# Neighbourhood-attention bias tables in an encoder block: key rows turned round, slots loaded in 13 transfers, tables built in the first stage

## The chip, the cores and the metric

One core of a Trainium2 chip runs the whole program in one launch. The metric is the device time in microseconds (us) of one execution; several executions are timed and their median is taken. A change of less than about 0.2% can't be told from none.

## What is computed

One layer of a bidirectional encoder on a prompt (1024 tokens) and a sample (512 tokens), each with 16 learned meta tokens before it. What matters here is the first attention group: 8 heads, tokens on a grid 64 wide, each query sees a window of 8 grid rows by 16 columns, with a learned bias by row and column offset, and the meta tokens.

```python
def _neighbourhood_attention(q, k, v, rpb, meta_bias):
    rows = n_real // GRID_W
    kh = min(NA_MAX_KH, rows)
    row_start = jnp.clip(r_idx - kh // 2, 0, rows - kh)
    col_idx = jnp.clip(c_idx - NA_KW // 2, 0, GRID_W - NA_KW)[:, None] + jnp.arange(NA_KW)
    col_off = col_idx - c_idx[:, None] + NA_KW - 1
    ...
    def row_fn(args):
        qr, r, rs = args
        ...
        row_off = rs + jnp.arange(kh) - r + NA_MAX_KH - 1
        bias = rpb[:, row_off[:, None, None], col_off[None]]
        ...
        s_loc = s_loc.astype(jnp.float32) * scale + bias[None]
        p = jax.nn.softmax(jnp.concatenate([s_loc, s_met], axis=-1), axis=-1)

def _layer(...):
    h = _rmsnorm(x, norm_mix)
    proj = h @ w_in
    ...    # neighbourhood heads | differential heads, output projection, residual
    x = x + _expert_choice_ffn(_rmsnorm(x, norm_ffn), ...)    # 16 experts, top-k tokens each
```

## The kernel before

Every engine has its instruction stream written out by hand, with semaphores between them; SyncE (SP) issues all transfers of the attention stages, in program order, and each of them is at least one instruction of its stream.

**Stage A (0 to 75 us).** The tokens come in 12 tiles of 128 rows (and one of 32), in pairs, in a loop: SP waits on `xn_ready` until both tiles of the pair before are normed, then loads `xt`; ScalarE squares, GpSimd makes the root, VectorE scales, TensorE turns the tiles round, ScalarE and VectorE split them into the parts `hT_hi` and `hT_lo`.

**Projections.** A unit is a pair of heads; units 0 to 3 are neighbourhood heads, 4 to 7 differential ones. `project` (L1427) makes V, Q and K of a unit in 12 chunks of 24 matmuls, in two PSUM banks by turns; `evac` (a helper at L650) copies each chunk out on ScalarE. Its weights come by `load_w` (L446), in three parts j = 0, 1, 2, and each part is split by `split_wq` on ScalarE (`wq_hi`) and then on VectorE (`wq_lo`, L980). Unit 0 is projected alone; each later unit during the attention of the unit before. On ScalarE `split_wq(1, 0)` stands between chunks 7 and 8 of unit 0; on ScalarE and VectorE `split_wq(1, 1)` stands ahead of the first attention step.

**Neighbourhood steps.** A unit has 13 steps (`NA`): three column groups `ct` (steps 0 to 2, 3 to 8, 9 to 11), each block of 16 query columns with three kinds of 8 grid rows, and a step for the meta tokens. In step s TensorE makes scores (L1471), half a chunk of the next unit's projection, turns the step before round (L1494, L1495), the other half chunk, and weights the values (L1508, L1515). VectorE adds the bias and finds the minimum of the negated sum (L1091, `nmax`), which waits for the bias slot; ScalarE takes the exponential (L751). In unit 3 VectorE also rotates the columns of unit 4 (L1036), from copies `swp` that SP issues (`swap_halves`, L524).

**Bias.** A slot (`bias[:, i % 2]`) holds, for one unit and column group, the bias of 128 queries against 384, 384 and 256 keys and 16 meta tokens. It is loaded from a DRAM table `window_bias` (8 heads x 3 groups x 16 columns x 32 rows x 32), by 31 transfers (L492) and three of `meta_bias` (L511, 128 partitions x 2 x 16 floats each). The table is filled with the mask value (L463, three transfers) and then written by 78 transfers of pieces of 16 floats from `rpb` (L481), after the last tile of stage A. Queries of 8 rows need 8 shifted row ranges; with key rows rising each shift is a transfer of its own.

Of the kernel before, what the change touches and what calls it, by code (L numbers as in the profile page):

```python
# [73 lines left out]
TROWS = 32  # L74
VCH = 24
SLOT_DMAS = 31 + 3
# [50 lines left out]
def build(nc, x_all, w_in, w_out, w_router, w_gate, w_up, w_down, rpb, meta_bias, lambdas, vecs,  # L127
# [7 lines left out]
    bias_h = nc.dram_tensor("window_bias", (NA_HEADS, 3, QW, TROWS * WIN), f32, kind="Internal")  # L135
    bias_d = bias_h.ap()

    ctx = ExitStack()
    with ctx:
# [165 lines left out]
        fill_ready, fill_in, diag_in = sem("fill_ready"), sem("fill_in"), sem("diag_in")  # L305
        mask_ready, bias_in = sem("mask_ready"), [sem(f"bias_in{b}") for b in range(2)]
# [76 lines left out]
        def window(tile, f, kind, block):  # L383

            base = (0, 4 * GRID_W, N_PROMPT)[kind]
            rows = tile[f, base:base + KROWS[kind] * GRID_W].rearrange("p (r k) -> p r k", k=GRID_W)
            return rows[:, :, WSTART[block]:WSTART[block] + WIN]
# [20 lines left out]
        def key_chunks(kind, block):  # L408

            first = (0, 1, 4)[kind]  # L410
            return [4 * (first + j) + block for j in range(KCOLS[kind] // P)]
# [17 lines left out]
        def _(sp):  # L429
# [6 lines left out]
            sp.dma_start(cos[:, :], rope[0]).then_inc(const_in, 16)  # L436
            sp.dma_start(sin[:, :], rope[1]).then_inc(const_in, 16)
            sp.dma_start(pmask[:, :], pair_mask).then_inc(const_in, 16)
# [12 lines left out]
            with sp.Fori(0, PAIRS) as i:  # L451
                for b in range(2):
                    sp.wait_ge(xn_ready, 2 * i + CREDIT)
                    sp.dma_start(xt[:, b, :], x_all[bass.ds((2 * i + b) * P, P), :]).then_inc(x_in[b], 16)
            sp.wait_ge(xn_ready, 2 * PAIRS + CREDIT)
            sp.dma_start(xt[0:TAIL, 0, :], x_all[N_REAL:NTOK, :]).then_inc(x_in[0], 16)


            flat = NA_HEADS * 3 * QW * TROWS * WIN
            sp.wait_ge(fill_ready, 1)  # L460
            for n in range(flat // (P * 1024)):
                dst = bass.AP(tensor=bias_h, offset=n * P * 1024, ap=[[1024, P], [1, 1024]])
                sp.dma_start(dst, mask_fill[:, :]).then_inc(fill_in, 16)  # L463
            sp.wait_ge(fill_in, 16 * (flat // (P * 1024)))
            CS = TROWS * WIN
            HS_ = 3 * QW * CS
            half = KW // 2
            runs = [(0, c, 1, 0, KW - 1 - c) for c in range(half)] + [(0, half, QW - half, 0, half - 1)]
            runs += [(1, 0, QW, 0, half - 1)]
            runs += [(2, 0, half + 1, half, half - 1)] + [(2, c, 1, KW, KW - 1 - c) for c in range(half + 1, QW)]  # L470
            for ct, c, n, k0, off in runs:
                for row0, nrow, roff in ((0, ROFF, 0), (ROFF + 1 + 3, KH, 3)):
                    dst0 = (ct * QW + c) * CS + row0 * WIN + k0
                    for h in range(NA_HEADS) if n > 1 else (None,):
                        if h is None:
                            src = bass.AP(tensor=rpb.tensor, offset=roff * COFF + off, ap=[[ROFF * COFF, NA_HEADS], [COFF, nrow], [1, KW]])
                            dst = bass.AP(tensor=bias_h, offset=dst0, ap=[[HS_, NA_HEADS], [WIN, nrow], [1, KW]])
                        else:
                            src = bass.AP(tensor=rpb.tensor, offset=(h * ROFF + roff) * COFF + off, ap=[[0, n], [COFF, nrow], [1, KW]])
                            dst = bass.AP(tensor=bias_h, offset=h * HS_ + dst0, ap=[[CS + 1, n], [WIN, nrow], [1, KW]])  # L480
# [58 lines left out]
            for i in range(2):  # L539
                load_bias(i)  # L540
# [1348 lines left out]
```

## Time and profile before

| | us |
|---|---|
| median of three runs | 3352.49 (3350.26 to 3354.61) |
| the profiled execution | 3356.26 |
| its span, first to last instruction | 3354.4 |

| engine | busy, us | share of the span |
|---|---|---|
| TensorE, matmuls | 3008.0 | 90% |
| VectorE | 1898.2 | 57% |
| ScalarE | 1475.6 | 44% |
| GpSimd | 171.3 | 5% |

The experts take the span from about 1200 us on, with TensorE busy 9 tenths or more in nearly every slice. The stages named above lie in the first 600 us. The table of 40 slices shows TensorE there at 3, 6 and 8 tenths in its first three slices of 84 us, then at 9; the granted clock of TensorE is below full in some of them. Read the waits for who waits for whom, then the timeline of each engine (start, duration, line, operation, and in brackets the idle time ahead with what ended it).

### The profile page before, as it was taken

To read this page: it belongs to the slowest core of one execution; us is meant where nothing else is said; L and a number is where in the kernel's file an instruction comes from. 1 tells how busy PE (TensorE), PEld (TensorE's weight loads), DVE (VectorE), ACT (ScalarE), POOL (GpSimd) and SP (SyncE) were. 2 spreads that over 40 slices of the span, in tenths; PEclk is the share of its full clock that TensorE was granted. 3 is DMA by queue.
4 is the path that set the end of the run, shared out by engine and by line. 5 is a ranking of instruction groups with operands and counts; after the bars stand their busy time and mean duration, and the time that the engine had idled before them with its cause. 6 is when DMAs were issued, how large, how long until landed. Compare 5 with 4: busy or idle time off the path is not lost.

```text
span 3354.4 us, 50481 instructions
## 1 busy us (share of the span) xinstructions
PE 3008.0 (90%) x19541; PEld 2809.8 (84%) x19541; DVE 1898.2 (57%) x2984; ACT 1475.6 (44%) x2422; POOL 171.3 (5%) x177
## 2 busy tenths in 40 slices
PE   3689998989898799179999999999999999999993
PEld 3678887768675577079999999999999999999993
DVE  5023223647567322856766676667667666766672
ACT  3023232323335222055655565556556555655562
POOL 1000000000000100000001000100100100000001
PEclk7889998989898789589999999999999999999996
DMA  4323332101001232077777787777777777877774
GB/s 131 56 57 73 73 73 55 30 27 34 21 23 59 85 125 97 3 233 234 236 228 237 224 249 222 237 233 232 234 232 239 224 237 228 248 220 234 237 218 171
DMA packets 649094, 529.21 MB, mean 158 GB/s; under 512 B 39792, under 2 KB 629904, under 8 KB 648880
## 3 DMA queue, kind: packets, MB, share of 16 engines
q1 hardware_dynamic: 640688, 500.53, 48.4%
q0 software_dynamic: 8192, 25.70, 3.9%
q8 instruction: 150, 2.46, 0.3%
q14 instruction: 64, 0.52, 0.0%
HBM read 473.45 MB, written 40.54 MB: 153 GB/s over the span
## 4 chain that ended last, share of the span: by engine, by line
PE 60%; issue 32%; DVE 3%; DMA 2%; POOL 1%; ACT 1%; SPq 0%; ACTq 0%; POOLq 0%; DVEq 0%
PE ps L1717 37%; PE ps L1718 17%; PE ps L1644 5%; DMA xt<-x_all_dram 1%; PE ps L1762 1%; DVE top_i L1285 1%; DVE top_v L1283 1%; DVE aff L1286 1%; PE ps L1711 1%; DMA raw<-w_up_dram 0%; PE ps L1662 0%; POOL rstd L1775 0%; DMA y_dram<-yo 0%; POOL rstd_d L1775 0%; DVE x L1225 0%
## 5 line engine op out<-in xcount | busy, mean ns | idle before, releaser
L1717 PE MATMUL ps<-xe,w_hi 128*128 128x392 f32 x4096 | 1195.3, 364 | 8.2 <-DVE xe L1328 8.2
L1718 PE MATMUL ps<-xe,w_lo 128*128 128x196 f32 x4096 | 1034.1, 252 | 0.0
L1315 DVE TENSOR_TENSOR w_lo<-raw,w_hi 128x2048 fp32r<-128x2048 f32 x384 | 875.8, 2284 | 11.3 <-ACT w_hi L650 11.3
L1718 PEld LDWEIGHTS ps<-xe,w_lo 128*128 128x128 f32 x4096 | 784.1, 191 | 0.0
L1717 PEld LDWEIGHTS ps<-xe,w_hi 128*128 128x128 f32 x4096 | 770.0, 188 | 8.5 <-DVE xe L1328 8.5
L650 ACT ACTIVATE w_hi<-raw 128x2048 fp32r<-128x2048 f32 x384 | 732.1, 1911 | 91.8 <-DMA raw<-w_gate_dram 75.1
L1717 PE MATMUL ps<-hid,w_hi 128*128 128x392 f32 x2048 | 609.4, 366 | 0.0
L1718 PE MATMUL ps<-hid,w_lo 128*128 128x196 f32 x2048 | 516.8, 252 | 0.0
L1718 PEld LDWEIGHTS ps<-hid,w_lo 128*128 128x128 f32 x2048 | 391.5, 191 | 0.0
L1717 PEld LDWEIGHTS ps<-hid,w_hi 128*128 128x128 f32 x2048 | 384.5, 188 | 0.0
L1348 DVE TENSOR_TENSOR gusum<-ps,part 128x392 f32<-128x392 f32 x256 | 145.0, 566 | 395.1 <-ACT part L650 395.1
L650 ACT ACTIVATE part<-ps 128x392 f32<-128x392 f32 x256 | 127.4, 498 | 511.3 <-PE ps L1718 511.3
L1427 PE MATMUL ps<-hT_hi,wq_hi 128*128 128x384 f32 (+1 forms) x768 | 287.1, 374 | 14.9 <-ACT kT L650 8.8
L1427 PE MATMUL ps<-hT_lo,wq_hi 128*128 128x384 f32 (+1 forms) x768 | 268.7, 350 | 0.0
L1427 PE MATMUL ps<-hT_hi,wq_lo 128*128 128x384 f32 (+1 forms) x768 | 268.2, 349 | 0.0
L779 ACT ACTIVATE e_df<-e_df,nmax 128x1040 f32<-128x1040 f32 (+3 forms) x112 | 112.3, 1004 | 214.7 <-DVE e_df L1164 214.7
L1427 PEld LDWEIGHTS ps<-hT_hi,wq_hi 128*128 128x128 f32 x768 | 149.9, 195 | 46.8 <-issue 28.6
L1369 DVE TENSOR_TENSOR yT<-ps,y_part 128x196 f32<-128x196 f32 x128 | 46.3, 361 | 198.1 <-ACT y_part L650 196.4
L650 ACT ACTIVATE y_part<-ps 128x196 f32<-128x196 f32 x128 | 42.3, 331 | 249.1 <-PE ps L1718 249.1
L1427 PEld LDWEIGHTS ps<-hT_lo,wq_hi 128*128 128x128 f32 x768 | 150.7, 196 | 0.3
L1427 PEld LDWEIGHTS ps<-hT_hi,wq_lo 128*128 128x128 f32 x768 | 149.9, 195 | 0.5
L1164 DVE TENSOR_SCALAR_CACHE_REDUCE e_df<-ps,nmm 128x1024 f32<-128x1024 f32 (+3 forms) x112 | 117.8, 1088 | 45.5 <-PE ps L1552 45.5
(166 smaller groups left out, 3212.2 us busy)
## 6 DMA issues: line engine op xcount, KB each, us to landing
raw<-w_gate_dram SPq DMA_DIRECT2D x128, 1024.0 KB, 5.3
raw<-w_up_dram SPq DMA_DIRECT2D x128, 1024.0 KB, 5.3
raw<-w_down_dram SPq DMA_DIRECT2D x128, 1024.0 KB, 5.5
wqkv<-w_in_dram SPq DMA_DIRECT2D x24, 512.0 KB, 4.0
xt<-x_all_dram SPq DMA_DIRECT2D x12, 512.0 KB, 4.2
v_na<-v SPq DMA_DIRECT2D x64, 96.0 KB, 2.3
mixed_heads<-mix SPq DMA_DIRECT2D x96, 64.0 KB
mixs<-mixed_heads SPq DMA_DIRECT2D x12, 512.0 KB, 4.8
```

The source lines that it names most:

```text
L650: return act.activation(out, in_, ACT.Copy, scale=scale)
L779: act.activation(e_df[0:rows, s % 2, c, 0:w], e_df[0:rows, s % 2, c, 0:w], ACT.Exp, bias=nmax[0:rows, s % 2, c:c + 1], scale=-1.0, accum_o ...
L1164: dve.tensor_scalar(e_df[0:rows, s % 2, c, 0:kt * P], ps[0:rows, 2 * c * BANK:2 * c * BANK + kt * P], -1.0, nmm[0:rows, c, t:t + 1], ALU.m ...
L1283: own.mark(dve.max(top, aff[:, :]))
L1285: own.mark(dve.max_index(top_i[:, 8 * r:8 * r + 8], top, aff[:, :]))
L1315: dve.tensor_tensor(w_lo[:, n % NW, :], raw[:, n % NRAW, :], w_hi[:, n % NW, :].bitcast(f32), ALU.subtract).then_inc(lo_done, 1)
L1348: dve.tensor_tensor(gusum[:, m % 2, :, :], src[:, :, 0:SLOTS], part[:, m % 2, :, :], ALU.add).then_inc(sum_done, 1)
L1369: dve.tensor_tensor(yT[:, d, :], ps[:, off:off + SLOTS], y_part[:, d % 2, :], ALU.add).then_inc(yT_done, 1)
L1427: ins = pe.matmul(ps[:, off:off + c1 - c0], wt[:, p, k, :], x[:, k, c0:c1], start=(k == 0 and j == 0), stop=(k == KD - 1 and j == 2))
L1644: ins = pe.matmul(ps[0:rows, off:off + 512], x[:, b, k, 0:rows], w[:, k, n * 512:(n + 1) * 512], start=(k == 0 and j == 0), stop=(k == KD ...
L1717: pe.matmul(out, w_hi[:, slot, cols], x.rearrange("p h n -> p (h n)"), start=first, stop=False)
L1718: return pe.matmul(out[:, 0:SLOTS], w_lo[:, slot, cols], x[:, 0, :], start=False, stop=last)
```

## The change

- K of the neighbourhood units is kept with its grid rows falling (`turned`): ScalarE copies a K chunk row by row, 6 copies of 64 columns in place of one of 384, with one more of 32 in the last chunk. Windows, value rows and `key_chunks` follow. The host turns `rpb`'s rows round and pads them.
- The shifts of 8 query rows are then a constant step in one table, so that a slot takes 5 pieces x 2 heads = 10 transfers and the 3 of `meta_bias`: 13 in place of 34.
- Two DRAM tables, `bias_full` and `bias_band`, take the place of `window_bias`. They are filled by 4 transfers ahead of the second pair of tiles, written by 5 transfers of 16-float pieces (3 after the third pair's loads, 2 after the fourth's) and one copy from table to table (after the last pair's).
- The masked part of a slot that no transfer writes is set once by a VectorE `memset` of both slots (128 x 4288) at the end of stage A.
- SP's order: the first pair's tiles ahead of `cos`, `sin`, `pmask` and the first weights; the loop of pairs is written out; both bias slots ahead of `load_w(1, 0)` and `load_windows(0, ...)` instead of behind them. VectorE and TensorE wait for 3 constants, VectorE for the other three later.

```diff
-SLOT_DMAS = 31 + 3
+SLOT_DMAS = 2 * 5 + 3
...
+            x_pair(0)
+            sp.dma_start(cos[:, :], rope[0]).then_inc(tables_in, 16)
+            sp.dma_start(sin[:, :], rope[1]).then_inc(tables_in, 16)
+            sp.dma_start(pmask[:, :], pair_mask).then_inc(tables_in, 16)
...
+            sp.wait_ge(fill_ready, 1)
+            for h, n, rows in FILLS:
+                dst = bass.AP(tensor=h, offset=n * 1024, ap=[[1024, rows], [1, 1024]])
+                sp.dma_start(dst, mask_fill[0:rows, :]).then_inc(fill_in, 16)
+            def diagonal(ct, c, n, k0, off):
+                src = bass.AP(tensor=rpb.tensor, offset=PADR * COFF + off, ap=[[0, n], [COFF, NA_HEADS * ROFF], [1, KW]])
...
+            half = KW // 2
+            for i in range(1, PAIRS):
+                x_pair(i)
+                if i == 2:
+                    sp.wait_ge(fill_in, 16 * len(FILLS))
+                    edge(0, 0, half, 0)
+                    diagonal(0, half, QW - half, 0, half - 1)
+                    diagonal(1, 0, QW, 0, half - 1)
+                if i == 3:
+                    diagonal(2, 0, half + 1, half, half - 1)
+                    edge(2, half + 1, QW - half - 1, KW)
+                if i == 5:
+                    sp.wait_ge(diag_in, 16 * DIAGS)
...
+                    sp.dma_start(dst, src).then_inc(band_in, 16)
...
+                def piece(table, rows, at_col, r0, nr, row0, nrow):
+                    for a in range(2):
...
+                        src = bass.AP(tensor=table, offset=(ct * QW * rows + first + row0) * WIN,
+                                      ap=[[WIN, nr], [rows * WIN, QW], [1, nrow * WIN]])
+                        dst = bass.AP(tensor=bias, offset=(QW * r0 * 2 + b) * 2 * SLOT + a * (SLOT + N_META) + at_col,
+                                      ap=[[4 * SLOT, nr * QW], [1, nrow * WIN]])
+                        sp.dma_start(dst, src).then_inc(bias_in[b], 16)
...
+                full(BOFF[0] + 4 * WIN, 0, 4, 0, KH)
+                band(BOFF[0], 4, 4, 0, 12)
+                band(BOFF[1], 0, 5, 0, 12)
+                full(BOFF[1], 5, 3, 5, KH)
+                full(BOFF[2], 0, QR, 0, KH)
...
+            sp.wait_ge(band_in, 16)
+            sp.wait_ge(bias_clear, 1)
+            for i in range(2):
+                load_bias(i)
             load_w(1, 0)
             for block in range(4):
                 load_windows(0, block)
-            for i in range(2):
-                load_bias(i)
             for j in range(1, 3):
                 load_w(1, j)
...
+                elif which == 1 and uu < UNITS:
+                    for r in range(6 * c, 6 * c + 6):
+                        at_k = turned(r) * GRID_W
+                        ins = copy(kTs[uu % 2][:, at_k:at_k + GRID_W],
+                                   ps[:, off + (r - 6 * c) * GRID_W:off + (r - 6 * c + 1) * GRID_W])
...
+            dve.memset(bias[:, :, :], MASKED).then_inc(bias_clear, 1)
+            dve.wait_ge(tables_in, 16 * 3)
```

How the change moves the instructions, in three places. SP at the start of the program, before (`mask_fill` and `rpb` pieces stand behind all tiles):

```order
L435 DMA lam_51<-lambdas_dram 128x256
L436 DMA cos<-rope_dram 128x1040
L437 DMA sin<-rope_dram 128x1040
L438 DMA pmask<-pair_mask_dram 32x128
L446 DMA wqkv<-w_in_dram 128x8x128 x3
...
L454 DMA xt<-x_all_dram 128x1024
...
L456 DMA xt<-x_all_dram 32x1024
L463 DMA window_bias<-mask_fill 128x1024 x3
L481 DMA window_bias<-rpb_dram 8x15x16
L481 DMA window_bias<-rpb_dram 8x8x16
```

The same place now:

```order
L452 DMA xt<-x_all_dram 128x1024 x2
...
L465 DMA wqkv<-w_in_dram 128x8x128 x3
...
L452 DMA xt<-x_all_dram 128x1024 x4
L489 DMA bias_full<-rpb_dram 8x127x16
L480 DMA bias_full<-rpb_dram 8x120x16
L480 DMA bias_full<-rpb_dram 16x120x16
L452 DMA xt<-x_all_dram 128x1024 x2
L480 DMA bias_full<-rpb_dram 9x120x16
L489 DMA bias_full<-rpb_dram 7x126x16
L452 DMA xt<-x_all_dram 128x1024 x4
L508 DMA bias_band<-bias_full 384x1x256
```

78 small transfers behind the tiles have become 5 larger ones and a copy between them. SP between stage A and the first attention step, before (31 rows of L492 in each slot; `v_87` is the value tile):

```order
L446 DMA wqkv<-w_in_dram 128x8x128
L533 DMA v_na<-v_87 32x6x128 x16
L492 DMA bias<-window_bias 16x2x256
L492 DMA bias<-window_bias 16x2x128
L492 DMA bias<-window_bias 16x2x384
...
L511 DMA bias<-meta_bias_dram 128x2x16 x3
...
L511 DMA bias<-meta_bias_dram 128x2x16 x3
L446 DMA wqkv<-w_in_dram 128x8x128 x2
L567 DMA mixed_heads<-mix 8x16x128
```

The same place now:

```order
L524 DMA bias<-bias_full 64x1x256 x2
L524 DMA bias<-bias_band 64x1x384 x2
L524 DMA bias<-bias_band 80x1x384 x2
L524 DMA bias<-bias_full 48x1x256 x2
L524 DMA bias<-bias_full 128x1x256 x2
L541 DMA bias<-meta_bias_dram 128x2x16 x3
...
L541 DMA bias<-meta_bias_dram 128x2x16 x3
L465 DMA wqkv<-w_in_dram 128x8x128
L564 DMA v_na<-v_87 32x6x128 x16
L465 DMA wqkv<-w_in_dram 128x8x128 x2
L600 DMA mixed_heads<-mix 8x16x128
```

The last two parts of unit 1's weights stood behind 68 bias transfers and now stand behind the value windows alone. ScalarE at the end of unit 0's projection, before:

```order
L650 ACTIVATE qT_78<-ps 128x32
L650 ACTIVATE wq_hi<-wqkv 128x512 x2
L650 ACTIVATE kT_80<-ps 128x384 x3
L650 ACTIVATE kT_80<-ps 128x416
L650 ACTIVATE wq_hi<-wqkv 128x512 x2
L751 ACTIVATE e_na,ssum<-e_na,nmax 128x400 x2
```

The same place now:

```order
L683 ACTIVATE qT_78<-ps 128x32
L683 ACTIVATE wq_hi<-wqkv 128x512 x2
L683 ACTIVATE kT_80<-ps 128x64 x24
L683 ACTIVATE kT_80<-ps 128x32
L683 ACTIVATE wq_hi<-wqkv 128x512 x2
L792 ACTIVATE e_na,ssum<-e_na,nmax 128x400 x2
```

Nothing changes its place there; four copies have become 25.

## Rows read from the trace of the kernel before

**Rows 1.** Waits, 70 to 200 us: engine, line, releaser; total us, times, longest us.

```profile
DVE wq_lo L980 <- ACT wq_hi L650: 77.9, 2, 49.4
ACT wq_hi L650 <- DMA wqkv<-w_in_dram: 52.8, 2, 37.8
PE ps L1471 <- DVE nmax L1091: 35.5, 1, 35.5
```

**Rows 2.** Timeline of SP, 0 to 200 us: start, us, line, transfer, count.

```profile
68.27 54.75 SPq L481 DMA_DIRECT2D window_bias<-rpb_dram  x78
124.44 0.41 SPq L446 DMA_DIRECT2D wqkv<-w_in_dram  x1
124.89 10.54 SPq L533 DMA_DIRECT2D v_na<-v  x16
135.48 15.86 SPq L492 DMA_DIRECT2D bias<-window_bias  x31
151.37 1.45 SPq L511 DMA_DIRECT2D bias<-meta_bias_dram  x3
152.87 14.46 SPq L492 DMA_DIRECT2D bias<-window_bias  x31
...
168.86 1.09 SPq L446 DMA_DIRECT2D wqkv<-w_in_dram  x2
```

**Rows 3.** Timeline of ScalarE: chunk copies of unit 0's projection.

```profile
108.55 0.55 ACT L650 ACTIVATE qT<-ps 128x256 f32<-128x256 f32 x2 [3.66 <-PE ps L1427]
113.10 0.58 ACT L650 ACTIVATE qT<-ps 128x384 f32<-128x384 f32 x2 [4.00 <-PE ps L1427]
...
141.11 0.52 ACT L650 ACTIVATE kT<-ps 128x416 f32<-128x416 f32 x1 [4.06 <-PE ps L1427]
```

**Rows 4.** Timeline of TensorE: projection's start and restart, scores of steps 0 to 3.

```profile
74.88 0.69 PE L1427 MATMUL ps<-hT_hi,wq_hi 128*128 128x384 f32 x1 [6.06 <-DVE hT_lo L973]
...
130.34 0.66 PE L1427 MATMUL ps<-hT_hi,wq_hi 128*128 128x384 f32 x1 [8.85 <-ACT kT L650]
...
141.68 0.92 PE L1471 MATMUL ps<-kT,qT 64*128 64x384 f32 x4 [0.61 <-ACT kT L650]
...
182.59 1.65 PE L1471 MATMUL ps<-kT,qT 64*128 64x384 f32 x4 [35.46 <-DVE nmax L1091]
...
193.79 0.70 PE L1471 MATMUL ps<-kT,qT 64*128 64x256 f32 x4
...
201.94 0.92 PE L1471 MATMUL ps<-kT,qT 64*128 64x384 f32 x4
```

**Rows 5.** Packets moved in 160:165, 533:538, 90:100 and 62.8:68.3 us, in that order.

```profile
DMA packets 917, 0.66 MB, mean 132 GB/s; under 512 B 320, under 2 KB 917, under 8 KB 917
...
DMA packets 540, 0.03 MB, mean 7 GB/s; under 512 B 540, under 2 KB 540, under 8 KB 540
...
DMA packets 2913, 0.18 MB, mean 18 GB/s; under 512 B 2912, under 2 KB 2912, under 8 KB 2912
...
DMA packets 480, 1.70 MB, mean 310 GB/s; under 512 B 64, under 2 KB 64, under 8 KB 480
```

**Rows 6.** Group of ScalarE, 70 to 600 us, by shape: busy us, mean ns.

```profile
L650 ACT ACTIVATE qT<-ps 128x128 f32<-128x128 f32 x8 | 2.1, 262 | 4.2 <-PE ps L1427 4.2
```

**Rows 7.** Timelines of SP and TensorE around unit 3: bias slots 10 and 11, a wait.

```profile
480.97 16.46 SPq L492 DMA_DIRECT2D bias<-window_bias  x31
...
516.88 14.58 SPq L492 DMA_DIRECT2D bias<-window_bias  x31
...
545.50 0.76 PE L1508 MATMUL ps<-v_meta,et_meta 32*128 32x128 f32 x2 [12.04 <-DVE et_meta L1079]
```

**Rows 8.** Timelines of VectorE and ScalarE in stage A: the mask, two pairs' squares.

```profile
2.07 0.91 DVE L941 MEMSET mask_fill<- 128x1024 f32 x1 [0.18 <-issue]
...
15.56 1.06 ACT L660 ACTIVATE junk<-xt 128x1024 f32<-128x1024 f32 x1 [5.38 <-DMA xt<-x_all_dram]
...
23.97 1.06 ACT L660 ACTIVATE junk<-xt 128x1024 f32<-128x1024 f32 x1 [6.02 <-DMA xt<-x_all_dram]
```

More of the change, by code:

```diff
@@ L408, in key_chunks, with turned @@
         def key_chunks(kind, block):
-            first = (0, 1, 4)[kind]
-            return [4 * (first + j) + block for j in range(KCOLS[kind] // P)]
+            groups = ((2, 1, 0), (3, 2, 1), (5, 4))[kind]
+            return [4 * g + block for g in groups]
+        def turned(row):
+            return PT * 2 - 1 - row if row < PT * 2 else PT * 2 + FULL * 2 - 1 - row
+        FILLS = [(h, n, min(P, np_ - n)) for h, np_ in ((full_h, 3 * QW * FROWS * WIN // 1024),
+                                                        (band_h, 3 * QW * NA_HEADS * BROWS * WIN // 1024))
+                 for n in range(0, np_, P)]
+        DIAGS = 5
         first_of = [min(s for s, x in enumerate(NA) if x[0] == ct) for ct in range(3)] + [NS]
@@ L465, in _ @@
[L465 to L480, printed above, removed]
-                        sp.dma_start(dst, src).then_inc(diag_in, 16)
@@ L482, in _ @@
[L482 removed]
             def load_bias(i):
                 u, ct, b = i // 3, i % 3, i % 2
[L488 to L506 removed]
+                def piece(table, rows, at_col, r0, nr, row0, nrow):
+                    for a in range(2):
+                        h = 2 * u + a
+                        first = PADR + h * ROFF if table is full_h else h * BROWS
+                        src = bass.AP(tensor=table, offset=(ct * QW * rows + first + row0) * WIN,
[3 more added lines that the diff above has]
+                        sp.dma_start(dst, src).then_inc(bias_in[b], 16)
@@ L507, in load_bias, with full, band @@
+                def full(*args):
+                    piece(full_h, FROWS, *args)
+                def band(*args):
+                    piece(band_h, NA_HEADS * BROWS, *args)
+                full(BOFF[0] + 4 * WIN, 0, 4, 0, KH)
[3 more added lines that the diff above has]
+                full(BOFF[2], 0, QR, 0, KH)
                 for kind in range(3):
@@ L699, in evac @@
                     copy(vT[:, 0:c1 - c0], ps[:, off:off + c1 - c0]).then_inc(pj_evac, 1)
+                elif which == 1 and uu < UNITS:
[3 more added lines that the diff above has]
+                                   ps[:, off + (r - 6 * c) * GRID_W:off + (r - 6 * c + 1) * GRID_W])
+                    if c == 3:
+                        ins = copy(kTs[uu % 2][:, N_REAL:NTOK], ps[:, off + N_REAL - c0:off + NTOK - c0])
+                    ins.then_inc(pj_evac, 1)
                 elif which == 1:
@@ L1871 @@
         "w_down": a["w_down"][0],
-        "rpb": a["na_rpb"][0],
+        "rpb": np.concatenate([np.zeros((PADR, 31), np.float32), a["na_rpb"][0][:, ::-1].reshape(-1, 31),
+                               np.zeros((PADR, 31), np.float32)]),
         "meta_bias": a["na_meta_bias"][0],
```

72 lines of the change are left out of this document (31 added, 41 removed).

## The prediction

> **What bounds the kernel now.** Most of the span is the experts' part with TensorE busy, which the change doesn't touch. So I read only the first 600 us, from the waits to the timelines. The waits between 70 and 200 us show one long hole on TensorE: 35.5 us in one piece, before the scores of step 1, released by VectorE's `nmax`. VectorE itself waited 49.4 us in `wq_lo` for ScalarE, and ScalarE 37.8 us for `wqkv` [rows 1]. The bias is not what they wait for: it is a weight transfer. SP's timeline tells why it is late: 78 table pieces take SP 54.8 us, then come one weight part, 16 window loads (10.5 us), 68 bias transfers (two slots of 31 at about 15 us and 3 at 1.45), and only at 168.9 the last two weight parts [rows 2]. SP's issuing is the bound from 68 to 170 us. Unit 0's projection, which stopped for the first weight part, shows the same queue: 8.85 us idle ahead of chunk 10, since ScalarE could copy no chunk while it waited for the part issued at 124.4 [rows 3, 4].
>
> **The first stall, step by step.** Now both slots are issued before the weights. They can start when VectorE's memset is done. The projection started at 74.9 [rows 4]; the memset follows at about that time on VectorE. An own figure for its length comes from the mask's 1024 columns below: 4288/1024 x 0.91 = 3.8 us, so SP goes on at about 78.7. Nothing waits for VectorE there until the first V chunk is turned. Each slot is then 10 transfers at 15.86/31 = 0.51 us and 3 in 1.45, 6.6 us of SP [rows 2]. Data: a slot is 2 x (64x256 + 64x384 + 80x384 + 48x256 + 128x256) floats = 0.93 MB; with a backlog, slot data moved at 132 GB/s, that is 7.1 us; the 768 pieces of `meta_bias` go at 540 in 5 us, another 7.1 us [rows 5]. Two slots: 78.7 + 1.9 + 28.4 = 109 us. `load_w(1, 0)` is behind them and lands at about 112, before ScalarE has copied chunk 7 (113.1 + 0.6) [rows 3]. Its wait disappears. `load_w(1, 1)` waits for chunk 7 (113.1) and is behind the windows (from 100.7 when V is done, 10.5 us), so it lands at about 117, needed at 132. `load_w(1, 2)` goes out at 130, needed at step 2.
>
> TensorE then runs on from 121.5. A chunk of 416 columns takes 113.10 - 108.55 = 4.55 us at full clock [rows 3], one of 384 then 4.2, and chunks 10 and 11 end at 130.3 in place of 141.07: **10.8 us**, of which 8.85 is the idle time and 2 the half clock after it. Step 0's scores wait for the last K copy: six copies of 64 columns and one of 32. A copy of 128 columns is 262 ns [rows 6] and one of 416 is 520 [rows 3], which is 0.9 ns a column, so 64 columns take 205 ns, 32 take 175, together 1.4 us in place of 0.5: **0.9 us lost**. The scores of step 1 follow 5.7 us later (141.68 to 147.4) and find VectorE ready: ScalarE splits until 133, VectorE until 133.7, step 0's minimum is there at 135.2, and TensorE comes at 137.5. The cover is 2.3 us. The **35.5 us** go. With them goes the low clock behind the hole: step 1 to step 2 took 193.79 - 182.59 = 11.20 us, step 2 to 3 took 8.15 [rows 4]: **3.1 us**. Sum: 10.8 + 35.5 - 0.9 + 3.1 = 48.5 us.
>
> **Later slots.** Ten more are loaded, one about every 36 us [rows 7]. SP needs 6.6 us for each in place of 17, which pays nothing where nobody waits for SP. One place waits: in unit 3 the copies `swp` and a weight part stand behind slot 11, and TensorE idles 12.04 us until 545.5 [rows 7]. Before, SP was through with the slot at 533.0 and its `meta_bias` data ended 7.3 us later, at 540.3. Now the data end at 516.9 + 1.9 + 7.1 + 7.3 = 533.2. **7.1 us** gained, all else in the same order. What is left of the hole, 5 us, is still followed by low clock; the hole of 8.85 us was, and I count no gain from it. Lower bound of this term 0; upper bound 12 with 4 for the clock.
>
> The 24 more K copies of units 1 to 3 lie in ScalarE's idle time ahead of each `et_na` copy, several us a step; uncovered they would cost 0.9 a chunk. The other K-side edits change no shape on TensorE: 0.
>
> **Stage A.** The first pair is loaded first, so its squares start some 8 us before 15.56. But the second pair was at 23.97 [rows 8], and its data now stand behind all that was in front of the first pair (tables, weights), the first pair itself (1.05 MB) and the fills (396 rows of 4 KB, 1.62 MB). At the fills' 310 GB/s [rows 5] this is 15.56 + 2.67/0.31 = 24.2 us. The early start is given back: **0**. From there the pairs go at their old pace of 8.4 us, if the table pieces stay out of the way. After the third pair come 8x127 + 8x120 + 16x120 = 3896 pieces of 64 B, after the fourth 1962. About 6 us of each pair's time is free of tile data. The old pieces went at 2912 in 10 us with the engines 26.8% busy, paced by SP's issuing [rows 5]. At that pace the first lot takes 13.4 us and costs 7, the second 6.7 and costs 1; at full use of the engines 3.6 us, and costs nothing. I take 0, since those engines were three quarters idle, and keep **8** as the bound. On the other side, if the fills overlap with loads better, 2 us gain.
>
> **Sum.** 48.5 + 7.1 = 55.6 us off 3354.4 gives a span of 3298.8, and off the median 3352.49 gives 3296.9. The profiled execution's own time (3356.26) is 1.9 over its span and 3.8 over the median; I apply the difference to the median.
>
> **A page against the trace.** The bias pieces now begin with dimensions of 4, 4, 5, 3 and 8 on the table's side, where the old ones had 16. The trace shows for `meta_bias` 108 packets a microsecond, and in the backlog of bias transfers 917 packets at 95.7% of 16 engines in 5 us, 84 ns each [rows 5]. The Trainium skill (DMA: Bandwidth & Descriptors, section "Why a DMA increments its semaphore by 16 and not by 1") says that a transfer is spread over the largest number of engines up to 16 that divides the slowest dimension of both sides, always the lowest-numbered ones. By it the first engine would carry 16 packets of each of the ten transfers. No row here shows which engine a packet used.
>
> **Rivals.**
> 1. *The slots' data become the bound of SP's queue, moderately.* If the ten transfers share few engines, so that one of them carries 160 of the 768 packets at 84 ns, a slot's data take 13.4 us, with `meta_bias` 20.5. Then the first weight part lands at 78.7 + 1.9 + 41 + 2.5 = 124, chunk 8 is copied at 127, and TensorE idles some 5 us with 2 of low clock; the unit 3 term shrinks to 0.8. Time: 3296.9 + 7 + 6.3 = 3310. For it: the narrow dimensions. Against: 84 ns was measured in a crush.
> 2. *The table pieces hold up the tiles.* If a piece costs what `meta_bias` costs (108 a us), the first lot takes 36 us and the second 18; less 6 each, 42 us: 3339. Against: the old `rpb` pieces, also read several times over, went nearly three times as fast without filling the engines.
> 3. *Slower.* The same mechanism as 1 at its end: all 768 packets of a slot on one engine, 64.5 us + 7.1. Slots are wanted every 36 us, so from 36 us a slot on the attention runs at the pace of the slots: twelve of 71.6 us from 78.7 end at 938 where 544 was forecast, some 3690. It decides below about 3 engines.
> 4. *The change moves the wait and gains nothing:* the weight part would still have to land at 179, for which I see no queue: 3352.
> 5. *More gain:* unit 3's hole shrinks under 3 us and its low clock goes too, 9 us more: 3288.
>
> **Chances.** Forecast 0.60, rival 1 0.22, rival 2 0.07, rival 3 0.03, rival 4 0.02, rival 5 0.06. Forecast's own ends: stage A +8/-2, unit 3 +7/-2, first stall 3 either way. The range 3286 to 3313 holds the forecast, rivals 1 and 5. A difference under 0.2% (7 us) can't be told from none. Faster by more 0.95, within 0.02, slower 0.03.
>
> **What would show it.** Right: no idle time over 2 us on TensorE between the projection's start and step 1, SP issuing `bias` from about 79 us, the step 1 scores at 136 to 139, a hole of about 5 us in unit 3, `hT_lo` of the last tile still near 74. Wrong: ScalarE waiting for `wqkv` ahead of chunk 8 (rival 1), tiles' squares more than 8.4 us apart after the third pair (rival 2), VectorE waiting for bias in every unit (rival 3).

## The result, and the profile after

| | before | after |
|---|---|---|
| median, us | 3353.55 (3350.26 to 3357.96) | 3297.18 (3294.05 to 3299.42) |
| profiled execution, us | 3356.26 | 3294.05 |
| its span, us | 3354.4 | 3292.2 |
| TensorE matmuls busy, us | 3008.0 | 2999.3 |
| VectorE, ScalarE busy, us | 1898.2, 1475.6 | 1901.7, 1482.0 |

The ratio of after to before is 0.9828 (95% interval 0.9815 to 0.984): 56 us less. The forecast was 3296.9. The profiled execution of after is its fastest one, 3.1 us under the median, while that of before was 3.8 over the median shown ahead; and 2.7 over that of its four runs; so the two spans differ by 62.2 us and the medians by 56.4. One of the six executions of the experiment `a_loads_spread` below took 10472 us at a granted clock of 0.255, and its figures are those of the other five. Lines of the code have moved: the scores' L1471 is now L1514, `window_bias` pieces (L492) are the slot pieces of L524, `evac` is L683.

**The first stall is gone.** The waits between 70 and 200 us (engine, line, releaser; total us, times, longest) have lost the second and third row of [rows 1], and the first has shrunk from 77.9 to 29.6 us. Of TensorE's waits the longest is now stage A's end, and none is for `nmax`; the rows that answer:

```profile
DVE wq_lo L1021 <- ACT wq_hi L683: 29.6, 2, 16.2
...
PE ps L1470 <- DVE hT_lo L1014: 6.1, 1, 6.1
...
PE ps L1514 <- ACT kT L683: 1.0, 1, 1.0
```

SP's timeline says why (start, us, line, transfer, count); it answers [rows 2]:

```profile
29.48 0.81 SPq L489 DMA_DIRECT2D bias_full<-rpb_dram  x1
30.34 4.30 SPq L480 DMA_DIRECT2D bias_full<-rpb_dram  x2
...
80.46 1.18 SPq L524 DMA_DIRECT2D bias<-bias_full  x2
81.69 2.64 SPq L524 DMA_DIRECT2D bias<-bias_band  x4
84.37 2.78 SPq L524 DMA_DIRECT2D bias<-bias_full  x4
87.19 2.41 SPq L541 DMA_DIRECT2D bias<-meta_bias_dram  x3
...
99.91 0.94 SPq L465 DMA_DIRECT2D wqkv<-w_in_dram  x1
102.66 13.92 SPq L564 DMA_DIRECT2D v_na<-v  x16
116.62 15.79 SPq L465 DMA_DIRECT2D wqkv<-w_in_dram  x2
```

Both slots are through by 99.9 us, 9.2 us of SP for the first; the first weight part goes out at 99.9 in place of 124.4, the last two from 116.6 (the 15.79 us hold a wait) in place of 168.9. ScalarE (start, us, line, operation; in brackets the idle time ahead) takes the first part without a wait, right after Q, and copies K in 64-column pieces; this answers [rows 3]:

```profile
114.86 0.58 ACT L683 ACTIVATE qT<-ps 128x384 f32<-128x384 f32 x2 [4.00 <-PE ps L1470]
115.32 1.15 ACT L683 ACTIVATE wq_hi<-wqkv 128x512 fp32r<-128x512 f32 x2
119.07 0.81 ACT L683 ACTIVATE kT<-ps 128x64 f32<-128x64 f32 x6 [2.59 <-PE ps L1470]
...
132.04 0.90 ACT L683 ACTIVATE kT<-ps 128x64 f32<-128x64 f32 x7 [3.74 <-PE ps L1470]
```

TensorE's timeline, the answer to [rows 4]: the projection's start, and the scores of steps 0, 1 and 2.

```profile
75.95 0.69 PE L1470 MATMUL ps<-hT_hi,wq_hi 128*128 128x384 f32 x1 [6.07 <-DVE hT_lo L1014]
...
132.99 0.92 PE L1514 MATMUL ps<-kT,qT 64*128 64x384 f32 x4 [0.98 <-ACT kT L683]
138.38 0.92 PE L1514 MATMUL ps<-kT,qT 64*128 64x384 f32 x4
...
146.76 0.70 PE L1514 MATMUL ps<-kT,qT 64*128 64x256 f32 x4
```

No gap stands before chunk 10 and none before step 1; what is left is the 0.98 us before step 0. From the projection's start to step 2's scores it is 146.76 - 75.95 = 70.8 us; before it was 193.79 - 74.88 = 118.9. That is 48.1 us gained, for 48.5 forecast. It isn't a lucky figure: in `after_again` (the changed kernel profiled a second time, below) the way from the projection's start to the end of unit 0's attention takes 232.44 - 80.31 = 152.1 us, and here 228.28 - 75.95 = 152.3.

**Unit 3** [rows 7]: SP with slot 11 and the first transfers behind it, VectorE's rotation, and TensorE's wait.

```profile
465.49 1.23 SPq L524 DMA_DIRECT2D bias<-bias_full  x2
466.77 2.69 SPq L524 DMA_DIRECT2D bias<-bias_band  x4
469.50 3.17 SPq L524 DMA_DIRECT2D bias<-bias_full  x4
472.70 1.83 SPq L541 DMA_DIRECT2D bias<-meta_bias_dram  x3
...
475.38 2.50 SPq L554 DMA_DIRECT2D swp<-qT  x4
```

```profile
483.72 0.56 DVE L1079 TENSOR_TENSOR qT<-qT,cos 128x384 f32<-128x384 f32 x1 [7.60 <-DMA swp<-qT]
```

```profile
486.82 0.45 PE L1551 MATMUL ps<-v_meta,et_meta 32*128 32x128 f32 x2 [2.25 <-DVE et_meta L1122]
```

The hole has shrunk from 12.04 to 2.25 us, 9.8 us where 7.1 were forecast. Behind the hole the clock is low for a while. Windows of 5 us with the granted clock in the third column from the right, of before behind its hole, of after behind its own, and of `after_again` behind a hole of 2.44 us:

```profile
545.00:550.00 5.00, 4.50 (x19) 3.55 (x19) 2.41 (x8) 1.71 (x5) 0.00 (x0) 0.50 0.21 56
550.00:555.00 5.00, 5.00 (x20) 4.75 (x21) 1.95 (x5) 0.00 (x0) 0.00 (x0) 0.60 0.14 37
```

```profile
487.00:492.00 5.00, 5.00 (x24) 4.12 (x24) 3.53 (x11) 1.71 (x5) 0.00 (x0) 0.66 0.18 49
```

```profile
492.40:497.40 5.00, 5.00 (x20) 4.00 (x21) 2.65 (x8) 1.71 (x5) 0.00 (x0) 0.50 0.21 55
497.40:502.40 5.00, 5.00 (x27) 4.84 (x26) 2.43 (x9) 0.49 (x1) 0.00 (x0) 0.83 0.18 47
```

At a clock of 0.50 and 0.60 before lost 2.5 + 2.0 = 4.5 us there, at 0.66 after loses 1.7: 2.8 us more in these two executions. That isn't an effect of the change. Windows of 5 us from the end of the wait give 2.5 + 0.9 = 3.4 us lost in `after_again`, 3.3 to 3.4 in three more profiles with holes of 2.4 to 2.6 us (`a_slots_behind`, `a_tables_late`, `a_loads_spread`), and 3.1 in `b_weights_first`, whose hole is still 11.91 us long. Over the whole of unit 3 (between TensorE's waits of 0.9 to 1.0 us for `et_meta` at its two ends) before takes 594.03 - 476.73 = 117.3 us and `b_weights_first` 116.6; after takes 532.96 - 428.17 = 104.8, and those four 106.2 to 106.5. So unit 3 gained 12.5 us in this pair of profiles and about 10.6 typically.

**Stage A.** ScalarE's squares of the second, third and fourth pair of tiles in after, and of the second pair in a second profiled execution of the same kernel (`after_again`):

```profile
23.88 1.06 ACT L693 ACTIVATE junk<-xt 128x1024 f32<-128x1024 f32 x1 [13.17 <-DMA xt<-x_all_dram]
...
32.44 1.06 ACT L693 ACTIVATE junk<-xt 128x1024 f32<-128x1024 f32 x1 [4.22 <-DMA xt<-x_all_dram]
...
42.15 1.06 ACT L693 ACTIVATE junk<-xt 128x1024 f32<-128x1024 f32 x1 [5.35 <-DMA xt<-x_all_dram]
```

```profile
27.77 1.06 ACT L693 ACTIVATE junk<-xt 128x1024 f32<-128x1024 f32 x1 [16.89 <-DMA xt<-x_all_dram]
```

The first pair's squares, at 8.3 us, come 7.3 us earlier than in [rows 8], the second at the old time: the early start is given back behind the fills, as forecast. The fourth pair comes 9.7 us after the third instead of 8.4, behind the first 3896 table pieces. The projection starts at 75.95 us, 1.1 later than before. But this execution is the lucky one. With stage A unchanged in after_again and three variants below that don't touch it (slots behind the weights, rows as transfers of their own, copies of `meta_bias`), the projection starts at 80.31, 78.12, 79.37 and 79.44 us; in two profiles with stage A as before, 74.88 and 75.43. So stage A costs about 4 us in a typical execution, not 0. (The profile of after_again is the slowest of its five executions, 12 us over their median, but the other three give the same start within 2.2 us.)

**The account.** 48.1 (first stall) - 1.1 (stage A) + 9.8 + 2.8 (unit 3) = 59.6 of the 62.2 us between the two spans. The rest lies in small changes of low clock at unit boundaries, which I can't attribute. A typical execution, with 4 us lost in stage A in place of 1.1 and 10.6 gained in unit 3, gives 48.1 - 4 + 10.6 = 54.7, and the medians 56.4; the 1.7 us between them are open.

### The profile page after: what moved, and what is told of

Same layout as the page of the kernel before. It is cut to its first block, busy times and chain, and to the rows that moved or that the text cites. A ratio compares the mean times of both kernels' runs of the same rounds, so it can differ in the third digit from the quotient of the medians.

```text
span 3292.2 us, 50201 instructions
## 1 busy us (share of the span) xinstructions
PE 2999.3 (91%) x19541; PEld 2802.1 (85%) x19541; DVE 1901.7 (58%) x2985; ACT 1482.0 (45%) x2506; POOL 168.6 (5%) x177
## 4 chain that ended last, share of the span: by engine, by line
PE 61%; issue 31%; DVE 3%; DMA 2%; POOL 1%; ACT 1%; SPq 1%; ACTq 0%; DVEq 0%; POOLq 0%
PE ps L1760 37%; PE ps L1761 17%; PE ps L1687 5%; DMA xt<-x_all_dram 1%; PE ps L1805 1%; DVE top_i L1328 1%; DVE top_v L1326 1%; DVE aff L1329 1%; PE ps L1754 1%; DMA raw<-w_up_dram 0%; PE ps L1705 0%; POOL rstd L1818 0%; DMA y_dram<-yo 0%; POOL rstd_d L1818 0%; DVE x L1268 0%
## 5 line engine op out<-in xcount | busy, mean ns | idle before, releaser
L1358 DVE TENSOR_TENSOR w_lo<-raw,w_hi 128x2048 fp32r<-128x2048 f32 x384 | 875.7, 2284 | 11.6 <-ACT w_hi L683 11.6
L683 ACT ACTIVATE w_hi<-raw 128x2048 fp32r<-128x2048 f32 x384 | 732.1, 1911 | 92.0 <-DMA raw<-w_gate_dram 75.3
L683 ACT ACTIVATE part<-ps 128x392 f32<-128x392 f32 x256 | 127.7, 499 | 510.5 <-PE ps L1761 510.5
L683 ACT ACTIVATE y_part<-ps 128x196 f32<-128x196 f32 x128 | 42.4, 331 | 249.1 <-PE ps L1761 249.1
```

The costliest lines, as they stand in the source:

```text
L683: return act.activation(out, in_, ACT.Copy, scale=scale)
L1358: dve.tensor_tensor(w_lo[:, n % NW, :], raw[:, n % NRAW, :], w_hi[:, n % NW, :].bitcast(f32), ALU.subtract).then_inc(lo_done, 1)
```

## The experiments

In each, the ratio is to the kernel before on the same chip; medians of different experiments are not all of one chip. Those named a_ start from the changed kernel, b_ from the one before.

**Is it the order?** The slots put back behind the first weight part and the windows.

```diff
-            for i in range(2):
-                load_bias(i)
             load_w(1, 0)
             for block in range(4):
                 load_windows(0, block)
+            for i in range(2):
+                load_bias(i)
             for j in range(1, 3):
```

> The changed kernel (span 3292.2, median 3297.2) with both bias slots issued where the kernel before had them: behind load_w(1, 0) and the 16 value windows, ahead of load_w(1, 1) and load_w(1, 2); 13 transfers a slot stay. Order theory (what paid in the first 190 us is that unit 1's weights no longer stand behind the slots): load_w(1, 1) goes out at about 134 in place of 117 and its data wait for the second slot's meta_bias pieces, so step 1's scores start near 147 in place of 138, a hole of some 9 us, and with the low clock behind it the time is 10 to 13 us longer, 3308 to 3310. Count theory (what paid is 26 transfers in place of 68): the slots take little of SP's time, the hole is under 3 us and the time is that of the changed kernel within 3 us.

Measured: 3311.98 us (3309.14 to 3313.01), ratio 0.9867 (0.985 to 0.9883). SP in its profile, and the scores of step 1:

```profile
135.82 5.65 SPq L465 DMA_DIRECT2D wqkv<-w_in_dram  x2
```

```profile
149.12 1.65 PE L1514 MATMUL ps<-kT,qT 64*128 64x384 f32 x4 [9.20 <-DVE nmax L1134]
...
159.91 0.70 PE L1514 MATMUL ps<-kT,qT 64*128 64x256 f32 x4
```

The hole before step 1 is back with 9.20 us, and step 1 to step 2 takes 10.8 us instead of 8.4. By the trace the order is worth 9.2 + 2.4 = 11.6 us with slots of 13 transfers. The medians differ by 14.8, the two ratios by 0.0039 or 13 us; stage A of this execution was 2.2 us later as well. The expectation's order theory (9 us of hole, 10 to 13 us in all) is borne out.

**The order alone, in the kernel before.** The last two weight parts ahead of the two slots; 34 transfers a slot and 78 table transfers stay.

```diff
-            for i in range(2):
-                load_bias(i)
             for j in range(1, 3):
                 load_w(1, j)
+            for i in range(2):
+                load_bias(i)
```

> The kernel before with one edit: load_w(1, 1) and load_w(1, 2) ahead of the two slots (68 transfers) in place of behind them. Order theory: step 1 then waits for the bias alone. The first weight part still waits for the table pieces (idle 8.9 us before chunk 10), load_w(1, 2) goes out when unit 0's projection is through (141), slot 0 is out at 158 and landed near 167: step 1's scores at about 169 in place of 182.6, the time 13 to 15 us shorter than before. Count theory (SP has the same number of transfers to issue before step 1 in either order): no change, within 3 us.

Measured: 3341.09 us (3339.43 to 3343.41), ratio 0.9954 (0.9937 to 0.9971), 15.8 us less than before. The two parts are issued at 136.0 instead of 168.9, but 33 us earlier gives only 15 of the hole, since VectorE then waits in step 0 for the slot itself, whose transfers are issued until 158.3:

```profile
136.00 5.55 SPq L446 DMA_DIRECT2D wqkv<-w_in_dram  x2
141.60 15.24 SPq L492 DMA_DIRECT2D bias<-window_bias  x31
```

```profile
DVE e_na L1091 <- DMA bias<-meta_bias_dram: 22.7, 1, 22.7
```

```profile
167.54 1.65 PE L1471 MATMUL ps<-kT,qT 64*128 64x384 f32 x4 [20.33 <-DVE nmax L1091]
```

The 8.85 us before chunk 10 stay too (8.71 here). So order alone can't clear the stall while 54.8 us of table transfers and 34 transfers of slot 0 stand ahead of the first step. How much of the 20.3 us each of these two holds up isn't shown: no run has 78 table transfers with short slots.

**Does the time of building the tables matter?** The five table transfers and the copy moved from between the pairs to behind the last tile.

```diff
                 x_pair(i)
-                if i == 2:
-                    sp.wait_ge(fill_in, 16 * len(FILLS))
-                    edge(0, 0, half, 0)
...
             sp.wait_ge(xn_ready, 2 * PAIRS + CREDIT)
             sp.dma_start(xt[0:TAIL, 0, :], x_all[N_REAL:NTOK, :]).then_inc(x_in[0], 16)
+            sp.wait_ge(fill_in, 16 * len(FILLS))
+            edge(0, 0, half, 0)
...
```

> The changed kernel with the five table transfers and the copy issued behind the last tile of stage A, in place of between the pairs. Cover theory: they take 10 to 14 us there (from 63 to about 76), the memset ends at 80.4 anyway, so the slots still start at 80 to 81; the fourth pair is no longer 1.3 us late, so the projection starts at 75 in place of 76.2 and the time is 0 to 2 us shorter. Rival: building the tables in the first stage is part of the gain, each of the six takes as long as in stage A (up to 4 us of SP) with two round trips, the slots start at 88 or later and load_w(1, 0) then lands after 120: 3 to 10 us longer.

Measured: 3300.04 us (3293.53 to 3302.8), ratio 0.9828 (0.981 to 0.9845), the same as after. The five transfers take SP 0.82 + 3.54 + 1.82 = 6.2 us instead of 54.8, and the copy is out before the memset of both slots is done:

```profile
65.17 3.54 SPq L480 DMA_DIRECT2D bias_full<-rpb_dram  x3
...
74.56 0.59 SPq L507 DMA_DIRECT2D bias_band<-bias_full  x1
81.01 1.16 SPq L521 DMA_DIRECT2D bias<-bias_full  x2
```

With 6 transfers in place of 78 nothing is lost where the 78 used to stand, so building the tables during stage A brings nothing. The projection started at 76.49 us, not at the 75 expected.

**How much does the number of slot transfers matter?** Each row of queries a transfer of its own for both heads, 27 in place of 13, same bytes, same order.

```diff
-                    for a in range(2):
-                        h = 2 * u + a
...
+                    for i in range(nr):
...
+                                      ap=[[rows * WIN, QW], [per * WIN, 2], [1, nrow * WIN]])
```

> The changed kernel with each piece of a slot cut into its query rows, both heads in one transfer: 24 + 3 = 27 transfers a slot in place of 13, each with 16 columns as its outer dimension; all orders stay. Order theory: unit 1's weights are still in time (slots out from 80 to 108, load_w(1, 0) lands near 118, load_w(1, 1) near 127, needed at 132), so no hole before step 1, or at most 2 us; in unit 3 SP needs 13.8 us for slot 11 in place of 9, the copies behind it come 4 to 6 us later, and the hole of 2.25 us grows to 6 to 8 us: with the clock 5 to 9 us longer, 3302 to 3306. Count theory: 27 is two thirds of the way back to 34, so of the 56 us some 35 are lost: 3332.

Measured: 3306.14 us (3299.07 to 3310.49), ratio 0.9844 (0.9823 to 0.9864). A slot takes SP 13.2 us, the first weight part goes out at 110.2, and still TensorE has no hole before step 1. The count is felt in one place, unit 3:

```profile
496.40 0.76 PE L1551 MATMUL ps<-v_meta,et_meta 32*128 32x128 f32 x2 [6.17 <-DVE et_meta L1122]
```

That is 3.9 us more hole than after's 2.25. The interval of the whole time overlaps that of after (0.9815 to 0.984), so this reading rests on the trace. The theory that the count of a slot's transfers carries the first stall (3332 us) falls, for 27 against 13.

**What is left of unit 3's hole: the `meta_bias` data?** Its 768 pieces (3 transfers, 2 heads, 128 partitions) read the same 16 floats of a head for all 128 partitions; here the host lays 128 copies in DRAM, so that each partition reads its own. Bytes, pieces and transfers are the same.

```diff
-                    sp.dma_start(dst, meta_bias[2 * u:2 * u + 2, :].partition_broadcast(P)).then_inc(bias_in[b], 16)
+                    sp.dma_start(dst, meta_bias[:, 2 * u:2 * u + 2, :]).then_inc(bias_in[b], 16)
...
-        "meta_bias": a["na_meta_bias"][0],
+        "meta_bias": np.repeat(a["na_meta_bias"], P, axis=0),
```

> The changed kernel with meta_bias handed over as 128 copies of its 8 x 16 floats, so that each partition's two pieces of 64 bytes are read from an address of its own; number, size and destination of the pieces stay (3 transfers of 256 a slot). Same-address theory (the 107 pieces a microsecond come from 128 reads of the same bytes): the 768 pieces of a slot go in 1 to 2 us in place of 7.2, what is queued behind them comes 5 to 6 us sooner, the hole of 2.25 us in unit 3 is gone (under 0.5) with its low clock: 3 to 5 us shorter than the changed kernel. Size theory (pieces of 64 bytes into 128 partitions are slow whatever is read): 107 a microsecond stay, no change.

> The changed kernel unchanged, as the measure for the three beside it. In four runs of one stage A the projection started at 76.2, 76.7, 78.4 and 79.7 us, by how fast the tiles came in; a run-to-run term of 2 to 3 us is expected in this kernel too: the start between 75 and 80, the rest of the span as before within 1 us, the median 3294 to 3302.

Measured: 3291.56 us (3288.58 to 3296.34), ratio 0.9802 (0.979 to 0.9815), beside 3296.32 (3294.88 to 3308.14), ratio 0.9819 (0.9806 to 0.9832), for the changed kernel again on the same chip. The intervals overlap; the trace decides. Packets moved during the meta pieces, in after (90 to 94 us) and then in a_meta_copies (477 to 480 us):

```profile
DMA packets 547, 0.13 MB, mean 32 GB/s; under 512 B 450, under 2 KB 547, under 8 KB 547
```

```profile
DMA packets 1195, 0.35 MB, mean 118 GB/s; under 512 B 854, under 2 KB 1195, under 8 KB 1195
```

Packets under 512 B go at 450/4 = 112 a us when all partitions read the same bytes, as in [rows 5]. When they read their own, 854 go in 3 us; as a slot has 768 pieces of `meta_bias`, some of these are others, and the pieces went at about 768/3 = 256 a us or more. The rotation in unit 3 follows slot 11's first issue (467.81) by 14.3 us instead of 18.2:

```profile
482.12 0.56 DVE L1079 TENSOR_TENSOR qT<-qT,cos 128x384 f32<-128x384 f32 x1 [3.88 <-DMA swp<-qT]
```

and no hole is left on TensorE there: unit 3 takes 531.32 - 430.62 = 100.7 us, where the changed kernel took 104.8 to 106.5. It was the common address, not the number of pieces.

**What does the first stage lose?** Fills behind the second pair's loads, `cos`, `sin`, `pmask` behind the fifth pair's.

```diff
-            sp.dma_start(cos[:, :], rope[0]).then_inc(tables_in, 16)
...
-            sp.wait_ge(fill_ready, 1)
-            for h, n, rows in FILLS:
...
                 x_pair(i)
+                if i == 1:
+                    sp.wait_ge(fill_ready, 1)
+                    for h, n, rows in FILLS:
...
+                if i == 4:
+                    sp.dma_start(cos[:, :], rope[0]).then_inc(tables_in, 16)
...
                 if i == 5:
```

> The changed kernel with the four fills issued behind the second pair of tiles and cos, sin and pmask behind the fifth, in place of ahead of the second pair. Volume theory (the early first pair gained nothing because 2.7 MB more stood ahead of the second pair): the second pair's squares start near 16.7 in place of 23.9, the pairs then follow at 8.4 us, the projection starts near 69 and everything behind it moves with it: 7 us shorter, median 3290. Rival (the pace of stage A is set by transfers whatever their order, total bytes over rate): the fills and tables then delay the third and sixth pair by what they spared the second, 0 to 2 us shorter.

Measured: 3290.06 us (3288.5 to 3295.3), ratio 0.9801 (0.9788 to 0.9814), 6.3 us under after_again. The second pair's squares are at 16.69 us, 7 earlier than in after, and some of it is lost again to fills and table pieces at the third and fourth pairs (26.95 and 36.80, 10.3 and 9.9 us apart in place of 8.4):

```profile
16.69 1.06 ACT L694 ACTIVATE junk<-xt 128x1024 f32<-128x1024 f32 x1 [6.25 <-DMA xt<-x_all_dram]
...
26.95 1.06 ACT L694 ACTIVATE junk<-xt 128x1024 f32<-128x1024 f32 x1 [5.19 <-DMA xt<-x_all_dram]
...
36.80 1.06 ACT L694 ACTIVATE junk<-xt 128x1024 f32<-128x1024 f32 x1 [5.41 <-DMA xt<-x_all_dram]
```

The projection starts at 70.80, where 69 was expected. Fills and tables were moved together, so what each of them cost isn't shown.

**Was the early first pair worth anything?** It goes back behind the tables and weights:

```diff
-            x_pair(0)
             sp.dma_start(cos[:, :], rope[0]).then_inc(tables_in, 16)
...
             for j in range(3):
                 load_w(0, j)
+            x_pair(0)
```

> The changed kernel with the first pair of tiles issued behind cos, sin, pmask and the three weight parts, as in the kernel before; the fills still stand behind it. Theory A (the forecast's step: the early first pair only moves the same bytes, and the second pair waits for all of them): the first pair's squares go from 8.3 back to about 15.6 us, the second pair's stay at 23.5 to 24.5, the projection starts within 1 us of the changed kernel's 76.2, and the time is 3296 to 3298. Theory B (the early first pair is worth its 7 us to stage A): second pair's squares at about 31, projection at 83, time about 3304. Theory C (bytes in another order help): second pair earlier than 23, time 3292.

Measured: 3302.45 us (3298.18 to 3304.68), ratio 0.9837 (0.982 to 0.9853). The first pair's squares are at 17.31 us, the second pair's at 27.01, the projection's start at 79.39:

```profile
27.01 1.06 ACT L693 ACTIVATE junk<-xt 128x1024 f32<-128x1024 f32 x1 [7.29 <-DMA xt<-x_all_dram]
```

Both lie inside what the changed kernel itself shows (second pair 23.88 and 27.77, start 75.95 and 80.31), and not at the 31 and 83 of the theory that it is worth 7 us. Theory A's own figures (23.5 to 24.5, start within 1 us of 76.2, 3296 to 3298) were missed too: it had left out the scatter of stage A. The interval of the ratio overlaps those of the changed kernel (0.9828 and 0.9819), and the time lies between the two theories. So the trace shows that no 7 us of the early start are left where the fills follow it; a few us can't be excluded.

**Both mends together**, fills and tables spread, and `meta_bias` from copies:

> The two edits together. Volume and same-address theories: 7 and 3 to 5 us add up, since they lie in different stages, 3285 to 3288. If one of the rivals holds, what the other edit gave alone.

Measured: 3283.94 us (3282.01 to 3286.8), ratio 0.9782 (0.9769 to 0.9795): 12.4 us under after_again, with the projection's start at 71.05 and no hole in unit 3. On another chip the same kernel was run again:

> a_spread_meta again, unchanged, for comparison on this chip: ratio to the kernel before 0.978, with stage A's start of the projection at 71 to 72, unless this execution scatters.

3287.57 us (3287.25 to 3289.43), ratio 0.9798 (0.9782 to 0.9814). It beats both kernels, by 2.0 to 2.2% against before and by 0.2 to 0.4% against the change.

**The same with the tables behind the last tile.**

```diff
                 x_pair(i)
-                if i == 2:
-                    sp.wait_ge(fill_in, 16 * len(FILLS))
-                    edge(0, 0, half, 0)
...
+            sp.wait_ge(fill_in, 16 * len(FILLS))
+            edge(0, 0, half, 0)
```

> The kernel a_spread_meta (fills behind the second pair, cos/sin/pmask behind the fifth, meta_bias from 128 copies in DRAM) with the five table transfers and the copy moved behind the last tile. Theory A: in a_spread_meta the table pieces behind the third and fourth pairs' loads hold up the fourth pair by 1.4 us beyond the 8.4 of a pair; without them the projection starts at about 70 instead of 71.4 and the tables are still there before the memset ends near 74, time 1 to 2 us less than a_spread_meta on the same chip. Theory B: the copy is now what the slots wait for (it was issued at 74.6 in the late variant with stage A ending 5.7 us later, so 69 here and done 1 to 2 us later), slots no later than 76, nothing gained or lost: 0. Theory C: the tables late push the slots and the first weight part past chunk 8: a hole before step 1 or chunk 8, 3 to 8 us more.

Measured: 3288.4 us (3283.61 to 3290.53), ratio 0.9794 (0.9778 to 0.9811), beside 3287.57 for a_spread_meta_2: no difference. In the profile the fourth pair comes at its 8.4 us again and the projection starts at 69.72 in place of 71.38. So theory A's start came and theory B's time, and the slots went out at 74.2, as soon as the memset was done, so B's reason (the copy holds them up) isn't what happened. Where the 1.7 us went stays open; they are smaller than the scatter of an execution.

## Why the prediction was right, and where it was not

- **What bounds the kernel: right.** The weight part behind SP's queue made the hole. The order put back brings 9.2 us of it back; the new order with the old tables and slots leaves 20.3. How the rest splits between fewer table transfers and shorter slots is argued from SP's timeline, not tested.
- **First stall, 48.5 us forecast, 48.1 measured.** Right in sum. Within it the K copies cost less than priced: six of 64 columns take 0.81 us and the last seven 0.90, where the steps put 1.4; TensorE waits 0.98 for the last one, 0.4 more than before and not 0.9. The step "64 columns take 205 ns" added up lengths of copies that overlap: here one of 64 columns lasts 230 ns (mean of 96), but six take 0.81, so the next starts (0.81 - 0.23)/5 = 0.12 us after it. Against this the projection itself took 132.01 - 75.95 = 56.1 us where before it was 141.07 - 74.88 = 66.2, 10.1 gained for 10.8 forecast: its 384-column matmuls follow each other every 0.32 us at the low clock and every 0.18 later, and the low clock lasts until 81.9 us in after and until 79.5 before, about 1.4 us longer from the projection's start.
- **SP's slots, mis-sized but covered.** "10 transfers at 15.86/31 = 0.51 us" gave 6.6 us a slot; they took 9.2 in the first (0.66 a transfer, and 2.41 for the three of `meta_bias`), starting at 80.5 for the forecast 78.7. The memset took 3.63 us (3.8 forecast), but starts at 76.74, after stage A's last work on VectorE, not with the projection. The weight part still landed early. The issues of 95 to 100 us with KB and us to landing show it:

```profile
wqkv<-w_in_dram SPq DMA_DIRECT2D x1, 512.0 KB, 9.7
```

  99.9 + 9.7 = 109.6, 5.7 us before ScalarE wanted it at 115.3.
- **Rival 1, few engines: the mechanism is there, its price is not.** With only slot data moving, from 83 to 88 us, the packets and the queue's share of 16 engines:

```profile
DMA packets 355, 0.49 MB, mean 98 GB/s; under 512 B 18, under 2 KB 354, under 8 KB 354
...
q1 hardware_dynamic: 354, 0.48, 32.7%
```

  32.7% of 16 engines is 5.2 engines, and 5 us x 5.2 / 354 = 74 ns a packet of some 1.4 KB. The Trainium skill (DMA: Bandwidth & Descriptors, section "Why a DMA increments its semaphore by 16 and not by 1") gives 4, 5, 3 and 8 engines for the slowest dimensions of these transfers; the 5.2 of the trace fit, though no row shows which engine a packet used. `a_rowwise` bears it out: its pieces have 16 as the slowest dimension, and where slot data are queued there (104 to 106 us) they fill the engines and move at 240 GB/s, where after had 98:

```profile
DMA packets 535, 0.48 MB, mean 240 GB/s; under 512 B 186, under 2 KB 534, under 8 KB 534
...
q1 hardware_dynamic: 534, 0.47, 92.5%
```

  The slot data went at 71 packets a us, 10.8 us a slot where 7.1 was forecast and 13.4 in the rival. What the rival had wrong is the queueing: it added up both slots' worst engine and all of `meta_bias` (weight part landed at 124; it was 109.6).
- **Unit 3, 7.1 us forecast, 12.5 measured in this pair and about 10.6 typically: the term that was mis-sized.** From the slot's first issue to the rotation it was 542.4 - 516.9 = 25.5 us before and is 483.7 - 465.5 = 18.2 now: 7.3, the step as computed, by the sum of SP time, data and `meta_bias` pieces. The step that failed is "all else in the same order". Slot 11 is now issued 19.1 us ahead of the moment at which TensorE comes to the wait (484.57), before 16.6 (533.46), since slot 10 no longer holds up the swaps in front of it (that cause is argued, not tested): 2.5 us. "I count no gain" from the clock was right in kind: behind holes of 2.4 to 2.6 us the clock cost as much as behind one of 11.91, and the 2.8 us of this pair are luck. Rival 5 (9 us more) went in this direction and was given 0.06.
- **Stage A, 0 forecast, about -4 typically.** The argument for the second pair (24.2 us) fits the fastest execution (23.88), not the typical one (25.7 to 27.8 in six profiles). Rival 2's sign came, but small: the fourth pair is 1.3 us late in after, and at its 8.3 us in `a_tables_late`, far from rival 2's 42. The new pieces went faster than the old ones' 2912 in 10 us: 3916 packets under 512 B from 33 to 38 us, with 16 engines 71.9% busy.
- So the total of 55.6 against 56.4 is partly luck: unit 3 gave about 3.5 more than forecast (5.4 in this pair) and stage A took about 4. Either alone would have moved the time inside the range.

## What to carry to other kernels

When an engine waits long for data whose transfer is short, read the issuing queue: what stands ahead of that transfer sets the time, and both shortening it (here 78 transfers to 6, and 34 a slot to 13) and moving the transfer ahead of it must be weighed. Here the shortening without the new order gave 45 us (`a_slots_behind`), the order without the shortening 16 (`b_weights_first`), and the two together 56. A transfer moved early only helps if the bytes behind it are not put in front of the next thing needed: here 2.7 MB of fills and tables ate 7 us until they stood behind later pairs. When a hole shrinks, don't count on the low clock behind it: here it cost 1.7 to 4.5 us whatever the hole's length (2.25 to 12 us), and went only with the hole. Profile one kernel twice before calling a few us in a stage an effect.

## What the runs showed of the hardware

- Pieces of 64 B that all partitions read from the same address in DRAM go at 108 to 112 a us (before, after) and hold up what is queued behind; from addresses of their own at about 256 a us or more (`a_meta_copies`). With 128 copies of the row the swaps behind a slot were ready 3.9 us sooner.
- Transfers with slowest dimensions of 4, 5, 3 and 8, though queued, kept 32.7% of 16 engines busy and moved 98 GB/s (after, 83 to 88 us); with 16 they kept 92.5% busy and moved 240 GB/s (`a_rowwise`, 104 to 106 us).
- Executions of one kernel differ by up to 4 us in when the second pair of tiles arrives (23.88 and 27.77 us) when 2.7 MB of fills and tables stand ahead of it; with stage A as before (23.97, 24.12), or with the fills behind the second pair (16.63 to 17.35 in four profiles), it stays within 1 us.
- The clock behind a hole on TensorE was low for 5 to 10 us after holes of 2.4 to 12 us alike, and took 3.1 to 4.5 us there; after one of 2.25 us it took 1.7.
- A copy of 64 columns on ScalarE lasts 230 ns, but one among its like starts 0.12 us after the one before.
